# Attention stage of a hybrid encoder layer: TensorE's work alternates head by head instead of four scores at a time

## The reference

```python
h = rms_norm(x, norm_gain) * (1 + scale[:, None]) + shift[:, None]
proj = h @ w_in
qa, ka, va, ga, qr, kr, vr, gr = jnp.split(proj, list(np.cumsum(sizes)[:-1]), axis=-1)
...
def row_step(args):
    r, q_r = args
    start = jnp.clip(r - kh // 2, 0, rows - kh)
    ...
    s = jnp.einsum('bhnqd,bhrnkd->bhnqrk', q_b, k_blk).astype(jnp.float32)
    s = s + bias[None]
    p = jax.nn.softmax(s.reshape(B, H, n_blk, NA_QBLK, kh * NA_KBLK), axis=-1).reshape(s.shape)
    o = jnp.einsum('bhnqrk,bhrnkd->bhnqd', p.astype(v.dtype), v_blk)
...
mix = jnp.concatenate([na, ret], axis=-1) @ w_out
return x + gate[:, None] * mix
```

## Time and profile before

| what | us |
|---|---|
| median of 3 runs (3400.47 to 3403.49) | 3400.68 |
| the profiled execution: its time | 3405.36 |
| the profiled execution: its span | 3403.2 |
| attention stage in it, first score to last value | 2139 to about 2852 |
| PE busy in 2139 to 2856 | 611.80 |
| DVE busy there | 353.10 |
| ACT busy there | 328.19 |

### The profile page before, as it was taken

One profiled execution on the slowest core, in us unless ns is written; L12 is line 12 of the kernel. 1 busy time (PEld: TensorE's weight loads), 2 busy tenths in 40 slices (PEclk: granted clock), 3 DMA queues, 4 the chain that ended last, 5 costly groups with the idle time before them and its releaser, 6 DMA issues. The chain is left out here.

```text
span 3403.2 us, 51074 instructions
## 1 busy us (share of the span) xinstructions
PE 3196.0 (94%) x17152; PEld 2701.2 (79%) x17152; DVE 1521.6 (45%) x3183; ACT 876.3 (26%) x1832; POOL 496.6 (15%) x462
## 2 busy tenths in 40 slices
PE   5999999999998999999999998588888886999999
PEld 1788888888877888888888887588787786888887
DVE  3343433334344333333333333354544555777775
ACT  2222222222232111111111111244444443111111
POOL 0111111111110000000000000222222211333332
PEclk8999999999999999999999999799999998999999
DMA  7444444444452222222222221965898573565554
GB/s 281 136 149 141 152 142 137 160 160 139 150 184 95 81 88 76 76 81 78 78 78 82 86 76 63 202 153 121 198 182 206 145 174 99 202 207 203 206 198 148
DMA packets 230405, 477.68 MB, mean 140 GB/s; under 512 B 30152, under 2 KB 104648, under 8 KB 227658
## 3 DMA queue, kind: packets, MB, share of 16 engines
q1 hardware_dynamic: 229196, 472.83, 45.7%
q0 software_dynamic: 1152, 4.19, 0.5%
HBM read 305.46 MB, written 171.47 MB: 140 GB/s over the span
## 5 line engine op out<-in xcount | busy, mean ns | idle before, releaser
L290 PE MATMUL proj<-w_att_hi,a_h_hi 128*128 128x512 f32 x2560 | 1025.9, 401 | 15.2 <-DVE a_h_lo L392 7.7
L290 PE MATMUL proj<-w_att_hi,a_h_lo 128*128 128x512 f32 x2560 | 1002.2, 391 | 0.0
L290 PE MATMUL proj<-w_att_lo,a_h_hi 128*128 128x512 f32 x2560 | 1000.7, 391 | 0.0
L290 PEld LDWEIGHTS proj<-w_att_hi,a_h_hi 128*128 128x128 f32 x2560 | 483.5, 189 | 108.0 <-DVE w_att_lo L266 8.4
L290 PEld LDWEIGHTS proj<-w_att_hi,a_h_lo 128*128 128x128 f32 x2560 | 482.3, 188 | 103.7
L290 PEld LDWEIGHTS proj<-w_att_lo,a_h_hi 128*128 128x128 f32 x2560 | 483.9, 189 | 92.6
L1285 PE MATMUL o_bank<-v_strip,probs_T 120*128 120x64 f32 x2560 | 340.7, 279 | 99.1 <-ACT probs_T L1148 99.1
L1285 PEld LDWEIGHTS o_bank<-v_strip,probs_T 120*128 120x128 f32 x2560 | 318.7, 196 | 124.7 <-ACT probs_T L1148 89.5
L1140 ACT ACTIVATE probs<-biased,neg_max 128x480 f32<-128x480 f32 x320 | 220.8, 690 | 318.8 <-PE t_bank L1272 218.5
L1109 POOL CAST q_block<-q_strip 128x512 fp32r<-128x512 f32 x80 | 48.9, 611 | 1626.0 <-DMA q_strip<-qT_d 1146.6
L1182 DVE CUSTOM_DVE_ANT_0 biased<-s_bank,bias_tables 128x480 f32<-128x480 f32 x320 | 197.9, 653 | 172.3 <-PE s_bank L1263 153.7
(11 more groups left out here) (131 smaller groups left out, 3521.9 us busy)
## 6 DMA issues: line engine op xcount, KB each, us to landing
k_strip<-kT_d SPq DMA_DIRECT2D x20, 1920.0 KB, 12.2
a_x<-in_x SPq DMA_DIRECT2D x40, 512.0 KB, 4.6
a_xT<-in_xT SPq DMA_DIRECT2D x40, 512.0 KB, 5.3
h_d<-a_h_hi SPq DMA_DIRECT2D x40, 512.0 KB, 2.7
h_d<-a_h_lo SPq DMA_DIRECT2D x40, 512.0 KB, 3.5
vg_d<-vg SPq DMA_DIRECT2D x40, 512.0 KB, 3.0
kT_d<-k_parts SPq DMA_DIRECT2D x80, 256.0 KB, 4.6
q_strip<-qT_d SPq DMA_DIRECT2D x40, 512.0 KB, 7.2
```

What stands on the lines that cost most here:

```text
L290: last = self.nc.tensor.matmul(bank, h[:, par, k, :], w[:, k, cols], start=(k == 0 and j == 0), stop=(k == KB - 1 and j == 2))
```

## The change

On TensorE the unit of four heads is given up. Each head step `j` issues score of j+4, turn of j+1 and value of j; turn 0 of the first unit goes ahead of the loop. The 80 units' instructions are the same in number and kind. On ScalarE take_out 0 and take_out 2 move ahead of exponentiate 4 and exponentiate 6. On VectorE take_out 1 moves ahead of add_bias 5, take_out 3 ahead of add_bias 7, and scale_unit follows add_bias 4. SyncE's and GpSimd's lists, the buffers and the counts of all semaphores stay.

```diff
             def unit(b, u, split=False):
                 j = GH * u
-                exponentiate(b, j + GH)
-                take_out(b, j)
-                exponentiate(b, j + GH + 1)
-                take_out(b, j + 2)
-                exponentiate(b, j + GH + 2)
-                exponentiate(b, j + GH + 3)
+                for k in range(GH):
+                    if k % 2 == 0:
+                        take_out(b, j + k)
+                    exponentiate(b, j + GH + k)
                 if split:
                     w_out.make_hi(act, u)
...
             def unit(b, slot, next_slot, u, first=False, split=False):
                 j = GH * u
-                for k in range(3):
+                for k in range(GH):
+                    if k % 2 == 1:
+                        take_out(b, j + k)
                     add_bias(b, next_slot, j + GH + k)
-                take_out(b, j + 1)
-                add_bias(b, next_slot, j + GH + 3)
-                if not first:
-                    scale_unit(b, u - 1)
-                take_out(b, j + 3)
+                    if k == 0 and not first:
+                        scale_unit(b, u - 1)
                 if split:
                     w_out.make_lo(dve, u)
...
-            def unit(b, u, last=False):
-
-                if not last:
-                    score(b, u + 1)
-                j = GH * u
-                turn(b, j)
-                turn(b, j + 1)
-                value(b, j)
-                turn(b, j + 2)
-                value(b, j + 1)
-                turn(b, j + 3)
-                value(b, j + 2)
-                value(b, j + 3)
+            def body(b, last):
+                for j in range(STEPS):
+                    if not last or j + GH < STEPS:
+                        score(b, j + GH)
+                    if not last or j + 1 < STEPS:
+                        turn(b, j + 1)
+                    value(b, j)
```

More of the change, by code:

```diff
@@ L1252, in _, with score @@
         def _(pe):
[L1253 to L1265, removed]
+            def score(b, j):
+                u, h = j // GH, j % GH
+                if h == 0:
+                    pe.wait_ge(q_placed, 2 * (UNITS * b + u + 1))
+                    if u % COLS == 0:
+                        pe.wait_ge(k_in[u // COLS % 2], 16 * (b + u // UNITS + 1))
+                at_least(pe, biased_made, STEPS * b + j - 3)
+                keys = k_strip[:, u // COLS % 2, h, :].rearrange("p (r w) -> p r w", w=W)
+                k0 = K0[u % COLS]
+                for part in range(2):
+                    last = nc.tensor.matmul(s_banks[h][:, 0:KEYS], q_block[:, u % 2, part, h, :],
+                                            keys[:, :, k0:k0 + KC], start=(part == 0), stop=(part == 1))
+                last.then_inc(scored, 1)
             def turn(b, j):
@@ L1288, in value @@
                 last.then_inc(valued, 1)
-            def unit(b, u, last=False):
-                if not last:
-                    score(b, u + 1)
-                j = GH * u
-                turn(b, j)
-                turn(b, j + 1)
-                value(b, j)
-                turn(b, j + 2)
-                value(b, j + 1)
-                turn(b, j + 3)
-                value(b, j + 2)
-                value(b, j + 3)
+            def body(b, last):
[5 more added lines that the diff above has]
+                    value(b, j)
             pe.wait_ge(first_in, 16 * QR)
-            score(0, 0)
+            for j in range(GH):
+                score(0, j)
+            turn(0, 0)
             with pe.Fori(0, BODIES - 1) as b:
[L1307 to L1310, removed]
+                body(b, False)
+            body(BODIES - 1, True)
 def out_stage(nc, x_tiles, w_out, ret_gain, gate_rows, decays, na_d, vg_d, part_d, qf_d, kv_d, gate_d, ident, exps,
```

## The result

The changed kernel takes 3781.1 us (median of 4 runs, 3779.6 to 3785.2) beside 3400.6 us for the kernel before: 1.112 times, 95% interval 1.110 to 1.114. The forecast was 3354.4, range 3330 to 3380. The profiled execution has a span of 3783.1 us.

The account below looks back on a forecast made before the run. The prediction took PE's list plus one exposed 1.30 us stall a unit as the bound. Gains of 42.3 and 9 us less 5 in the last body, 46.3 from 3400.7, gave 3354.4 us, range 3330 to 3380.

Parts of the forecast that it names:

- the stall of 1.30 us: Kernel before, ahead of value 0: PE stands still once a unit; without it 8.48 us would be about 7.18.
- PE's own work and the chain: Per unit: PE's list 7.04 us; the chain through ScalarE, 3.78 us per two heads, decides, giving 7.56.
- The last body: Split of `w_out` no longer hidden: a unit takes 9.21 us against 8.48, 5 us lost over 7 units.
- Bodies 3 to 5: SyncE's list is full there, PE waits for key strips; gain only 9 us where 24 units would give 22.
- The forecast's lower end, 3341: Whole kernel: lower end of the forecast's 3341 to 3373, from the ends of the unit and of bodies 3 to 5.
- the first unit waits for bias tables either way and counts as nothing: Stage start: the first unit was given no gain or loss in the sum.
- the term for a unit, 7.56 us: Attention stage: a unit takes 0.92 us less than 8.48; over 46 units at full clock 42.3 us won.
- The paragraph on the clock: Attention stage: shorter stops, about 0.26 us twice a unit, leave the clock at 1.00; no term in the sum.
- lower clock outside places where PE had stopped: New profile: one of the listed signs that would show the prediction wrong; no size given.
- Rival 4: Attention stage: the clock swings between its levels, 136 us longer, 3490 us; chance 0.02.
- Rivals 1 to 3: Strips alone set bodies 3 to 5, 3363 or 3373 (0.20); PE's list bounds, 3331 (0.08); costlier handing-over, 3439 (0.09).
- rival 3: Two-head chain: handing over costs more per link; 0.14 more each gives a unit of 8.96, total 3439; chance 0.09.

Follow-up runs that it names:

- the fours: Changed kernel with the next unit's four scores together, turn 0 issued ahead of value 3, and VectorE's old list: 3331.0 us.
- the burst: Changed kernel with each head's two score matmuls issued 8 times over for four head steps of the first body (56 more matmuls): 3575.1 us.

## Why the prediction was wrong

**Bounds of the kernel before, and the stall of 1.30 us:** right. It was exposed, and a list that hides it takes 1.54 us less a unit where the clock allows (6.94 us with the fours).

**PE's own work and the chain:** right, at the high level. Forecast 7.56 a unit with a wait ahead of even values; 3.78 for two heads in the run with the burst, where the weight loads wait 0.19 to 0.20 us for the forecast's 0.26. At the low level, where the changed kernel is, the chain is hidden.

**The last body:** right at the high level, 9.21 forecast, 9.10 in the run with both helps, the first three units in fours and the earlier q and k loads (ScalarE's part at 2730.34 and 2739.44). Not foreseen was that these stops can bring the clock down. The forecast's lower end, 3341, leaves these 5 us out: with a unit of 7.46 and bodies 3 to 5 at their best it is 3346.

**Bodies 3 to 5:** right in kind. PE waited 5.6 and 6.9 us for strips where it ran head by head at the high level, for values' strips and not for keys'. The fours, which are faster, waited for both. What these waits cost at a fast pace is measured between the fours with and without the earlier loads: 30 us, the low level behind the waits included. Right only as a few us of waiting, wrong as a price, since the level behind them was not counted.

**The step that failed is the one where the sum takes its durations.** PE's part of the links and the 1.76 us of its list are rows of stretches at full clock, and "the first unit waits for bias tables either way and counts as nothing" carried them to a stage that starts at the low level. The stage's first units counted for everything. Before, the group of eight scores at 2170.82 raised the clock behind the last stop, and the change takes that group apart. So the term for a unit, 7.56 us, measured 13.44: PE's list takes 3.36 us a head step at a clock of 0.50, and the chain of 3.78 for two heads, which was to decide, is hidden under it. The paragraph on the clock asked only what could bring the level down, and compared stops of PE: 1.30 us once with 0.26 twice a unit. On that question it was right, since the head-by-head order kept 1.00 for 600 us in the run with both helps. It didn't ask what would bring the level up. The changed kernel is at the low level with no stop at all, the "lower clock outside places where PE had stopped" that the prediction itself names as a sign of being wrong.

The paragraph also misread the row with 0.82. It says that no wait of PE stands in the list there. Two of the 76 waits do (PE's waits in 2741 to 2760):

```profile
PE o_bank L1285 <- ACT probs_T L1148: 2.1, 2, 1.1
```

The first ends at 2747.2, the clock falls at 2749.4, and it is back at 2756.2, in the next group of eight scores. Read so, the row shows both that a stop of 1.06 us is sometimes followed by a fall and that the scores standing together bring the level back, and the change takes these scores apart.

**Rival 4** had the right engine and the right symptom but another mechanism and 0.02 of the chance. Its price, 3490 by a swinging clock, was also short: the level does not swing, it stays. The Trainium skill, TensorE: Matmul & The Clock Gate, section "A second HAM failure mode: psum-queue depth-cycling", puts such a loss down to short idle times between groups that make the clock swing; here the head-by-head order whose weight loads stop for 0.2 us every second head held 1.00 for 280 us with the burst, and for the 500 us of the window with both helps, and the one with no stop held 0.50 for 1000 us. The measurement decides: in this kernel it was not the idle times that kept it low.

**Rivals 1 to 3** were about tens of us; none is what happened. For rival 3 (links 0.09 us longer) the burst's 3.78 us is the answer: they are not.

What stays open: why the alternating order does not bring the level back. Groups of eight and of four score matmuls did, single scores of two matmuls between a value and a turn didn't, and twice the level rose with no group of scores ahead. A score differs from a turn and a value also in its shape, and no run varied grouping and shape apart. Nor is it settled which stop ends the level: behind 5.6, 6.9 and 2.2 us the head-by-head order went on low, stops near 1 us did it in a few of many cases, and one of 1.4 us in the fours passed.

## What to carry to other kernels

Before a reorder is costed with durations at full clock, look at which level the stage starts, and at what PE did just before each rise in the trace; if the change takes those instructions apart, price the stage at the low level too. An order that holds the clock may not be able to reach it. In this kernel the remedy was a group of scores at the stage's start and the removal of the waits for transfers behind it, or a group again behind each wait. And when PE is busy all the time, look at the granted clock before believing that nothing is wrong.

## What the hardware showed that was not expected

- The same order of the same instructions has two lasting paces: 1.89 us a head step at a granted clock of 1.00, held for 500 us, and 3.36 us at 0.50, held for 1000 us, both with PE busy 99% or more.
- What happened at the start decides: three units of eighty, at the start, changed the total by 445 us (3781.0 to 3335.7).
- 640 matmuls more made the kernel 349 us faster (3432.4 against 3781.1).
- In the head-by-head order the level fell behind single waits of 5.6 and 6.9 us and stayed low for 525 us and more. In the kernel before, three stops of 1.06 to 1.18 us among some 76 had a fall behind them, and each was made good within the next group of eight scores.
